# Two more waits of GpSimd for VectorE in the norm ahead of each feed-forward stage, and the first pair's weight sums ahead of a gate product

## What is computed

```
# layer 0: gated short convolution; layer 1: forgetting attention
x = layer_norm(ALPHA * x + mixer(x), g, b)                 # norms 0 and 2
x = layer_norm(ALPHA * x + swiglu(x, w_gu, w_down), g, b)  # norms 1 and 3

def layer_norm(x, g, b):
    mu  = mean(x);  var = mean((x - mu) ** 2)
    return (x - mu) * rsqrt(var + 1e-5) * g + b

def swiglu(x, w_gu, w_down):
    g, u = split(x @ w_gu, 2)
    return (silu(g) * u) @ w_down                          # hidden width 2816
```

## Time and profile before

| what | value |
|---|---|
| median of 3 runs | 2687.68 us (2683.68 to 2688.5) |
| the profiled execution | 2684.62 us, of it span 2682.6 us |
| busy: TensorE, VectorE, ScalarE, GpSimd | 94%, 50%, 34%, 39% of the span |
| chain that ended last | TensorE 77%, VectorE 8%, DMA 5% |
| mean granted TensorE clock | 0.972 |

### The profile page before, as it was taken

One profiled execution on the slowest core, in us unless ns is written; L12 is line 12 of the kernel. 1 busy time (PEld: TensorE's weight loads), 2 busy tenths in 40 slices (PEclk: granted clock), 3 DMA queues, 4 the chain that ended last, 5 costly groups with the idle time before them and its releaser, 6 DMA issues.

```text
span 2682.6 us, 48004 instructions
## 1 busy us (share of the span) xinstructions
PE 2527.8 (94%) x17611; PEld 2459.2 (92%) x17611; DVE 1344.1 (50%) x2439; ACT 914.7 (34%) x1751; POOL 1047.6 (39%) x709
## 2 busy tenths in 40 slices
PE   8999997999999999979999899989799999999996
PEld 8999987999999999869999788879699999999995
DVE  2222257433333766655265677752763433456656
ACT  3111125333333211233222677651543333321123
POOL 2222244644444222433322666644554444432233
PEclk9999998999999999989999999989899999999998
DMA  3111111222222222104478877741022222232211
GB/s 112 47 47 47 47 41 27 77 86 71 78 84 87 109 82 113 49 8 158 158 260 301 254 203 193 209 130 40 24 72 90 83 63 88 84 108 92 91 73 64
DMA packets 215261, 271.50 MB, mean 101 GB/s; under 512 B 13959, under 2 KB 169607, under 8 KB 214140
## 3 DMA queue, kind: packets, MB, share of 16 engines
q1 hardware_dynamic: 207004, 236.90, 27.6%
q0 software_dynamic: 8160, 33.30, 4.0%
HBM read 205.68 MB, written 64.51 MB: 101 GB/s over the span
## 4 chain that ended last, share of the span: by engine, by line
PE 77%; DVE 8%; DMA 5%; issue 3%; POOL 3%; ACT 3%; SPq 2%; POOLq 0%; DVEq 0%; ACTq 0%
PE ps L2525 24%; PE ps L2526 24%; PE ps L2527 24%; DMA ncb<-ccum 1%; DMA o_t<-oe 1%; PE ps L2927 1%; DVE zl L2033 1%; PE ps L2912 1%; PE ps L2909 1%; DVE ln_qb L1876 1%; PE ps L2945 1%; DMA kp<-cache_k 1%; PE ps L2944 1%; DVE ln_qb L1878 1%; DVE traw L2127 1%
## 5 line engine op out<-in xcount | busy, mean ns | idle before, releaser
L1002 POOL TENSOR_TENSOR pair_lo<-pair_raw,pair_hi 128x512 fp32r<-128x512 f32 x240 | 314.6, 1334 | 437.9 <-ACT pair_hi L1365 405.3
L2525 PE MATMUL ps<-xh,whi 128*128 128x344 f32 x1320 | 433.1, 328 | 25.7 <-POOL xl L913 10.7
L871 POOL TENSOR_TENSOR wlo<-wraw,whi 128x1024 fp32r<-128x1024 f32 x91 | 220.9, 2430 | 583.0 <-ACT whi L1245 424.6
L2526 PE MATMUL ps<-xl,whi 128*128 128x344 f32 x1320 | 426.3, 323 | 0.0
L2527 PE MATMUL ps<-xh,wlo 128*128 128x344 f32 x1320 | 425.9, 323 | 0.0
L2525 PE MATMUL ps<-th,pair_hi 128*128 128x258 f32 x1280 | 361.6, 282 | 2.4 <-ACT pair_hi L1365 1.0
L2527 PE MATMUL ps<-th,pair_lo 128*128 128x258 f32 x1280 | 361.8, 283 | 0.0
L2526 PE MATMUL ps<-tl,pair_hi 128*128 128x258 f32 x1280 | 361.1, 282 | 0.0
L2026 DVE TENSOR_TENSOR x<-x,ps 128x344 f32<-128x344 f32 x432 | 215.8, 511 | 170.6 <-PE ps L2527 169.9
L2525 PE MATMUL ps<-zh,whi 128*128 128x344 f32 x864 | 286.0, 331 | 6.8 <-DVE zl L2485 5.6
L2525 PEld LDWEIGHTS ps<-xh,whi 128*128 128x128 f32 x1320 | 252.2, 191 | 33.4 <-POOL xl L913 11.7
(11 more groups left out here) (311 smaller groups left out, 5689.5 us busy)
## 6 DMA issues: line engine op xcount, KB each, us to landing
pair_raw<-ffn_w_gu SPq DMA_DIRECT2D x80, 512.0 KB, 4.9
zraw<-z_t SPq DMA_DIRECT2D x22, 1032.0 KB, 5.8
z_t<-zout SPq DMA_DIRECT2D x20, 1032.0 KB, 6.5
kp<-cache_k SPq DMA_DIRECT2D x32, 512.0 KB, 5.8
vp<-cache_v SPq DMA_DIRECT2D x32, 512.0 KB, 5.7
wraw<-a_w_in SPq DMA_DIRECT2D x24, 512.0 KB, 3.7
even_raw<-ffn_w_down SPq DMA_DIRECT2D x20, 512.0 KB, 3.7
wraw<-ffn_w_down SPq DMA_DIRECT2D x20, 512.0 KB, 6.1
```

Source lines behind the costliest of these rows:

```text
L871: pool.tensor_tensor(lo, raw, f32(hi), ALU.subtract).then_inc(w_lo, 1)
L1002: pool.tensor_tensor(pair_w[q]["lo"][k], pair_w[q]["raw"][k], f32(pair_hi[k][:, :]), ALU.subtract).then_inc(p["wlow"], 1)
L2525: pe.matmul(out, w_h, m_h, start=start, stop=False, skip_group_check=onto)
L2526: pe.matmul(out, w_h, m_l, start=False, stop=False, skip_group_check=onto)
```

## The change

In the GpSimd stream two waits are added: for all sums of squares of the chunks 0 and 1 (dsum 6) ahead of the third weight split, and for those of chunk 2 (dsum 9) ahead of the two rebuilds. It holds for norm 0 and norm 2. In the VectorE stream of each feed-forward stage the first pair's weight sums are cut in two: three of them (`first_sums`) go ahead of the gate product of chunk 2, the fourth (`last_sum`), whose place is that of a weight block still in use, behind it and behind a wait for the last of the three blocks. Before, all four came behind two low parts and T_3. ScalarE gets a wait for the four T sums ahead of the first `save_m1`.

```diff
                 ln_squares_sum(i, 1)
+                pool.wait_ge(*ln[i].at("dsum", 3 * 2))
                 low(n + KB + 2, n + KB + 2)
                 ln_squares_sum(i, 2)
                 ln_low(i, 1, 0, KB)
+                pool.wait_ge(*ln[i].at("dsum", 3 * NCH))
                 odd_whole(i // 2, 0)
                 odd_whole(i // 2, 1)
...
                     u = 2 * i
+                    if first:
+                        act.wait_ge(*p.at("tsum", 4))
                     save_m1(u)
...
                 def weight_sums(u, i, q):
+                    first_sums(u, i, q)
+                    last_sum(u, q)
+
+                def last_sum(u, q):
                     raw = pair_w[q]["raw"]
+                    dve.wait_ge(*p.at("wsum", 4 * u + 3))
+                    dve.tensor_tensor(raw[M_S4], raw[M_N1K2], raw[M_S2], ALU.subtract).then_inc(p["wsum"], 1)
+
+                def first_sums(u, i, q):
+                    raw = pair_w[q]["raw"]
+                    n1k1, n2k2, n2k1 = raw[M_N1K1], raw[M_N2K2], raw[M_S3]
                     dve.wait_ge(*p.at("ab"[q], 32 * (i + 1)))
-                    if isinstance(u, int) and u == 0:
-                        dve.wait_ge(full[NCH - 1], g0 + 3)
                     dve.tensor_tensor(raw[M_S1], n2k1, n2k2, ALU.add).then_inc(p["wsum"], 1)
...
                 t_sum(T_4, x21, traw[T_2][:, :, :], ALU.subtract)
+                first_sums(0, 0, 0)
                 first_product(2)
+                dve.wait_ge(full[NCH - 1], g0 + 3)
+                last_sum(0, 0)
                 t_low(T_2, 1)
                 t_sum(T_3, x22, x12, ALU.subtract)
                 t_low(T_1, 2)
-                weight_sums(0, 0, 0)
```

More of the change, by code:

```diff
@@ L2134, in weight_sums @@
                 def weight_sums(u, i, q):
+                    first_sums(u, i, q)
+                    last_sum(u, q)
+                def last_sum(u, q):
                     raw = pair_w[q]["raw"]
-                    n1k1, n1k2, n2k2, n2k1 = raw[M_N1K1], raw[M_N1K2], raw[M_N2K2], raw[M_S3]
+                    dve.wait_ge(*p.at("wsum", 4 * u + 3))
[3 more added lines that the diff above has]
+                    n1k1, n2k2, n2k1 = raw[M_N1K1], raw[M_N2K2], raw[M_S3]
                     dve.wait_ge(*p.at("ab"[q], 32 * (i + 1)))
-                    if isinstance(u, int) and u == 0:
-                        dve.wait_ge(full[NCH - 1], g0 + 3)
                     dve.tensor_tensor(raw[M_S1], n2k1, n2k2, ALU.add).then_inc(p["wsum"], 1)
@@ L2144, in weight_sums @@
                     dve.tensor_tensor(raw[M_S2], raw[M_S1], n1k1, ALU.subtract).then_inc(p["wsum"], 1)
-                    dve.wait_ge(*p.at("wsum", 4 * u + 3))
-                    dve.tensor_tensor(raw[M_S4], n1k2, raw[M_S2], ALU.subtract).then_inc(p["wsum"], 1)
                 def form(u, dst, n, t, mult, a, b):
```

## The result

The changed kernel takes 2668.68 us (median of 4, 2666.56 to 2673.07), the kernel before, run beside it, 2685.68 us. The ratio is 0.994 with a 95% interval of 0.9925 to 0.9954, that is 12 to 20 us less. The forecast was 14.3 us less. The profiled execution took 2673.07 us, span 2671.4, the slowest of the four.

A forecast was written before the change was run, and what follows sets the result against it. TensorE, busy 94% of the span, was taken as the bound, so only its waits could be won: 3.5 + 0.9 + 4.2 + 5.1 + 0.6 = 14.3 us, giving 2673.4 against 2687.68 us, range 2667 to 2680.

The forecast's parts named there:

- second wait: GpSimd wait ahead of the rebuilds: chunk 2's broadcast starts 4.2 us sooner in layer 0, 5.1 in layer 1.
- weight sums: Three sums ahead of the gate product: first pair starts 1.15 us sooner, 0.3 us a layer kept, bounds -0.75 and 1.9.
- What is held up, and by what: In the norms, a GpSimd operation under way holds up a VectorE operation with two SBUF inputs until it ends.
- First wait: GpSimd wait ahead of the third weight split: chunk 1's variance starts sooner, 3.5 us won in layer 0, 0.9 in layer 1.
- The step from 2.0 to 3.5, the clock: Layer 0, chunk 1, variance to broadcast: a shorter wait avoids the slow clock, 1.5 us more, bounds 0 and 1.5.
- The moved split: Layer 0's third weight split ends near 410.5, not 409.6, hidden by 0.8 us before the block needing it.
- the rebuilds' length: Chunk 2's two rebuilds take 7.05 us, from 428.85 to about 435.8 in layer 0, over VectorE's next chain.
- Half clock behind the new wait: After chunk 2's broadcast, 24 matmuls might run at half rate: nothing in the sum, 0.8 us a layer in the range.
- A: Rival: VectorE's small 86x4 operations are not held by chunk 2's rebuilds; gain 20.0 us, 2667.7; chance 0.12.
- B: Rival: chunk 1 clock gain missed (1.5), half clock after broadcasts (1.6), last part 2.1 lower; gain 9.1, 2678.6; chance 0.20.
- C: Rival: VectorE's sums of squares are long for their own inputs, not for GpSimd; no gain, 2687.7; chance 0.04.
- D: Rival: first pair's load lands late, delaying gate product and fourth block; 2693.5 us at 9 us late; chance 0.04.

The follow-up runs named there:

- no_rebuild: Kernel before with GpSimd's two rebuilds of odd rows cut from 344 to 8 columns each, no wait added: 2666.72 us, ratio 0.9939.
- wait1_only: Kernel before with only the GpSimd wait ahead of the third weight split added: ratio 0.9978.
- sums_only: Changed kernel without its two GpSimd waits, keeping the early weight sums and ScalarE's wait: ratio 1.0009 to the kernel before.
- wait2_only: Kernel before with only the GpSimd wait ahead of the two rebuilds added: ratio 0.9971.
- after: The changed kernel as first measured, all edits on the kernel before: 2668.68 us, ratio 0.994.
- after_again: The changed kernel measured once more, all edits on the kernel before: 2672.55 us, ratio 0.9951.
- waits_only: Kernel before with both GpSimd waits and nothing else: 2672.41 us, ratio 0.9961.
- split_first: Changed kernel with VectorE waiting for GpSimd's split of the fourth weight block before the T sum T_4: 2673.14 us, ratio 0.9957 to the kernel before.
- diag_wait: Changed kernel with GpSimd's wait ahead of the rebuilds put later, until VectorE has written the diagonal: 2666.89 us, ratio 0.9934 to the kernel before.

## Why the prediction was right

The sum, 14.3 us, agrees with what the two stages won in both traces of the changed kernel (14.1 and 14.5) and lies within the intervals of both measurements. That it agrees to 0.2 us is luck in part: the second wait won 1.5 us more than forecast in the two layers together, and the pair's columns, with the weight sums and the clock, gave 0.8 to 1.5 less (and chunk 1 another 0.8 less in the first trace). The steps were right in kind, and their errors cancelled. By its steps:

- *What is held up, and by what.* Shown: no_rebuild removes the slowness without a wait, the waits remove it without removing work.
- *First wait.* Forecast 3.5 and 0.9 us, wait1_only 3.7 and 1.2. The step from 2.0 to 3.5, the clock, came true: the lead grows from 2.0 us at the variance (410.02 to 408.02) to 3.6 at the broadcast (416.64 to 413.08) in that trace. In the first trace of the changed kernel layer 0 won 2.5, for a reason upstream of the change. Against sums_only or wait2_only, where the clock was low for longer, layer 0's 3.7 would have been some 5 us. The moved split cost nothing, as said: no trace has a wait at the block that needs it.
- *Second wait.* Forecast 4.2 and 5.1, measured 5.0 and 5.8 in every kernel that has it. The mechanism was the one forecast, down to which two operations are held (1.72 and 3.04 us, forecast 2 and 3.3) and which is not. The mis-sized term is the rebuilds' length: I took 7.05 us from the earlier trace rows, where VectorE's sum of 128x688 had its turn between the two, and they take 6.20 where only an 86x4 operation does. That is the 0.8 us.
- *Half clock behind the new wait.* Taken as nothing in the sum, with 0.8 us a layer as the bound. Ten stages have the new wait of 2.58 us without the later one (two layers of after, after_again, waits_only, wait2_only and split_first). In seven the clock stayed at 2.4 GHz, as from 434 to 441 above. In three it fell: layer 0 of after_again, layer 0 of wait2_only (0.79 from 433 to 441) and layer 1 of waits_only.

```profile
432.53 1.51 PE L2586 MATMUL ps<-ln_g,one 86*128 86x344 f32 x2 [2.58 <-DVE ln_g L1909]
...
432.00:440.00 8.00, 7.47 (x27) 0.57 0.00 0
...
1920.00:1927.00 7.00, 6.76 (x22) 0.51 0.00 0
```

  The first two lines are from after_again, the last from waits_only. In these three the lead shrinks by 0.8 to 1.0 us from the broadcast to the next block, in the seven by 0.1. So the bound had the right size, and "nothing" was right in seven cases of ten. The page "TensorE: Matmul & The Clock Gate" of the Trainium skill (section "HAM oscillation — how this bites in real kernels") warns of recurring waits; the trace agrees in the three stages and not in the seven, with the same wait in all. What decides between them was not tried.
- *Weight sums.* Forecast 0.3 us a layer, measured 0.0 and 0.2 in sums_only, within the scatter. Each piece was there: the new wait (0.49, forecast 0.75), the old one gone, the T_3 low part ending 25.5 us after the fourth block's start where it was 25.8. The wait moved from the pair's start to its fifth product.
- *Rivals.* A was refuted as a forecast of this change (3.04 us and not 0.16), and its price, 2.8 us a layer more, was then had by diag_wait. Of B's parts, the half clock came in three stages of ten, and its whole never. C and D did not come: the rebuilds start behind L1885, and no wait of VectorE on a load stands at the weight sums.

Not forecast: the lost turn before the fourth block in layer 1, 2.3 us at its place and nothing in the end. The load lands later there by 0.7 us; why was not tried.

## What to carry to other kernels

Look for operations of VectorE and GpSimd that end together: in these rows the one that began later was held. A wait that lets the short one on the critical path go first can be worth more than faster code, but follow the chain to its end, since the long operation lands on the next link; here the right place was after the whole chain (2.8 us a layer more than after its first part). A wait that vanishes at one matmul and stands again a few products on (1.89 us at the pair's first, 1.94 at its fifth) has won nothing; measure the lead at a matmul well behind the edit.

## What the runs showed that was not expected

VectorE and GpSimd took turns one for one even where VectorE's operations had no wait between them: with splits pending, T_3 took 3.41 us instead of 2.3 (460.84), the low part behind it 3.40 instead of 2.29, and GpSimd's six splits 13.24 us instead of 7.53. The Trainium skill (page "SBUF — State Buffer", section "SBUF: two separate sides") has the shared port pair as a lock held for the whole instruction by whoever starts first; the trace agrees for each single pair (430.06 to 433.10 behind a rebuild that ends at 433.08) and adds the order: in each of these places the engine that waited was next, though more work stood queued behind the holder. The reciprocal of 86x4 with one input ran in 0.17 us beside a rebuild (428.10), where the operation with two inputs behind it was held. Two inputs are not the whole condition that the prediction made of it: its own row at 1126.89 is an operation with one SBUF input, and it was held for 2.27 us.
